# Twelve modulation sums moved from VectorE to GpSimd

## What is computed

```python
def ada_modulate(x, c, norm_g, ada_w, ada_b):
    ada = jax.nn.silu(c) @ ada_w + ada_b          # (1,1024) @ (1024,3072), per layer
    shift, scale, gate = jnp.split(ada, 3, axis=-1)
    h = rmsnorm(x, norm_g) * (1.0 + scale[:, None, :]) + shift[:, None, :]
    return h, gate[:, None, :]

def even_layer(...):
    h, gate_res = ada_modulate(x, c, norm_g, ada_w, ada_b)
    a, u, v, gate = _split(h @ in_w, EVEN_SIZES)
    ya = pool_mixer(a, pool_w, pool_scale)
    yb = spatial_gating(u, v, sgu_norm_g, sgu_w, sgu_b)
    y = jnp.concatenate([ya, yb], axis=-1) * jax.nn.silu(gate)
    return x + gate_res * (y @ out_w)

def odd_layer(...):
    h, gate_res = ada_modulate(x, c, norm_g, ada_w, ada_b)
    gq, gk, gv, glr, sq, sk, sv, gate = _split(h @ in_w, ODD_SIZES)
    ...
```

## Time and profile before

| | |
|---|---|
| median of three runs | 932.27 us (930.97 to 932.85) |
| the profiled execution's own time | 932.22 us |
| its span, first to last instruction | 930.4 us |
| mean granted TensorE clock | 0.994 |
| busy: TensorE / VectorE / ScalarE / GpSimd | 911.9 / 656.7 / 510.3 / 5.8 us |

### The profile page before, as it was taken

One profiled execution on the slowest core, in us unless ns is written; L12 is line 12 of the kernel. 1 busy time (PEld: TensorE's weight loads), 2 busy tenths in 40 slices (PEclk: granted clock), 3 DMA queues, 4 the chain that ended last, 5 costly groups with the idle time before them and its releaser, 6 DMA issues.

```text
span 930.4 us, 19535 instructions
## 1 busy us (share of the span) xinstructions
PE 911.9 (98%) x8637; PEld 887.2 (95%) x8637; DVE 656.7 (71%) x780; ACT 510.3 (55%) x612; POOL 5.8 (1%) x21
## 2 busy tenths in 40 slices
PE   8999999999999999999999999999999999999998
PEld 7999998999999999999998999899899999999998
DVE  3977888785668567767779876557777674465565
ACT  4446353445644567864595663376666553454445
POOL 1000000000000000000000000000000000000000
PEclk9999999999999999999999999999999999999999
DMA  9999457875576634467534443334444566566421
GB/s 337 363 348 322 155 182 263 280 241 171 181 232 221 191 127 137 136 234 227 180 120 149 137 142 92 92 92 148 137 158 137 182 203 215 175 190 215 159 91 46
DMA packets 153559, 172.30 MB, mean 185 GB/s; under 512 B 4152, under 2 KB 137812, under 8 KB 153348
## 3 DMA queue, kind: packets, MB, share of 16 engines
q1 hardware_dynamic: 152032, 168.48, 55.9%
q10 hardware_dynamic: 1220, 2.53, 0.8%
q0 software_dynamic: 224, 0.05, 0.0%
HBM read 170.00 MB, written 1.05 MB: 184 GB/s over the span
## 4 chain that ended last, share of the span: by engine, by line
PE 71%; DVE 12%; ACT 8%; issue 5%; DMA 4%; SPq 0%; DVEq 0%; ACTq 0%
PE pj L2772 57%; DVE w_lo L1557 3%; ACT w_hi L1063 2%; DVE cst_phase L1531 2%; DMA raw<-in_even_in_w_dram 1%; DMA raw<-in_ada_w_dram 1%; PE pj L2724 1%; DMA spare<-in_even_in_w_dram 1%; PE pj L2726 1%; PE pj L2725 1%; PE m_all L2189 1%; PE pj L2555 1%; PE m_all L2462 1%; PE m_all L2445 1%; DMA raw<-in_even_out_w_dram 1%
## 5 line engine op out<-in xcount | busy, mean ns | idle before, releaser
L1557 DVE TENSOR_TENSOR w_lo<-raw,w_hi 128x2048 fp32r<-128x2048 f32 (+2 forms) x129 | 287.9, 2236 | 127.9 <-ACT w_hi L1063 127.2
L2772 PE MATMUL pj<-h_hi,w_hi 128*128 128x256 f32 x1160 | 328.9, 284 | 2.5 <-issue 2.4
L2772 PE MATMUL pj<-h_lo,w_hi 128*128 128x256 f32 x1160 | 323.8, 279 | 0.0
L2772 PE MATMUL pj<-h_hi,w_lo 128*128 128x256 f32 x1160 | 323.7, 279 | 0.0
L1063 ACT ACTIVATE w_hi<-raw 128x2048 fp32r<-128x2048 f32 (+2 forms) x129 | 240.1, 1864 | 53.4 <-PE pj L2772 23.2
L2772 PEld LDWEIGHTS pj<-h_hi,w_hi 128*128 128x128 f32 x1160 | 217.3, 187 | 6.4 <-issue 5.1
L2772 PEld LDWEIGHTS pj<-h_lo,w_hi 128*128 128x128 f32 x1160 | 217.4, 187 | 0.3
L2772 PEld LDWEIGHTS pj<-h_hi,w_lo 128*128 128x128 f32 x1160 | 217.3, 187 | 0.2
L2772 PE MATMUL pj<-y_lo,w_hi 128*128 128x256 f32 x624 | 175.0, 280 | 0.0
L2772 PE MATMUL pj<-y_hi,w_hi 128*128 128x256 f32 x592 | 166.7, 282 | 2.7 <-DVE w_lo L1557 1.9
L2772 PE MATMUL pj<-y_hi,w_lo 128*128 128x256 f32 x592 | 165.8, 280 | 0.0
(11 more groups left out here) (433 smaller groups left out, 1144.9 us busy)
## 6 DMA issues: line engine op xcount, KB each, us to landing
raw<-in_odd_in_w_dram SPq DMA_DIRECT2D x28, 1024.0 KB, 5.2
raw<-in_w_in_dram SPq DMA_DIRECT2D x23, 1024.0 KB, 5.3
raw<-in_ada_w_dram SPq DMA_DIRECT2D x21, 1024.0 KB, 6.4
raw<-in_w_ff_in_dram SPq DMA_DIRECT2D x16, 1024.0 KB, 5.4
raw<-in_w_ff_out_dram SPq DMA_DIRECT2D x16, 1024.0 KB, 5.2
raw<-in_even_in_w_dram SPq DMA_DIRECT2D x12, 1024.0 KB, 5.5
raw<-in_even_out_w_dram SPq DMA_DIRECT2D x8, 1024.0 KB, 6.3
raw<-in_odd_out_w_dram SPq DMA_DIRECT2D x8, 1024.0 KB, 5.4
```

The costliest lines, as they stand in the source:

```text
L1557: V.tensor_tensor(lo[:, 0:n], raw_of(u)[:, 0:n], hi[:, 0:n].bitcast(F32), ALU.subtract).then_inc(done, 1)
L2772: m = nc.tensor.matmul(to, a_, b_, start=(s == 0 and q == 0 and (fb == 0 or not together)), stop=(s == len(steps_) - 1 and q == 2), skip_g ...
```

## The change

A12 to A23 are summed on GpSimd. Where VectorE scaled and added a row block in one instruction, GpSimd is given two: a `tensor_scalar` that multiplies the block in place in `raw`, and a `tensor_tensor` that adds it to `acc`. The first block of an even unit is written to `acc` directly, so an even unit takes seven instructions and an odd one eight, 90 in all; each waits for the one ahead by a new semaphore `ada_pool`. VectorE loses 48 instructions. The SP queue and TensorE wait for `ada_pool` where they waited for `ada_acc`.

```diff
--- before.py
+++ after.py
@@ -48,7 +48,8 @@
 PAD = max(WINDOWS)
 ADA_PE = (0, 2, 4)
 ADA_K, ADA_N = 4, 512
-ADA_DVE = [n for n in range(24) if n not in ADA_PE]
+ADA_POOL = list(range(12, 24))
+ADA_DVE = [n for n in range(24) if n not in ADA_PE and n not in ADA_POOL]
 GLA_H, GLA_C, GLA_TAU = 4, 64, 16.0
 SB_H = 8
 AT_G, AT_H, HD = 3, 4, 64
@@ -724,6 +725,17 @@
             else:
                 eng.wait_ge(S("p_lo"), PLE_LO[un["own"]])
 
+        def ada_pool_ops(n):
+
+            return sum(2 * ADA_K - (m % 2 == 0) for m in ADA_POOL if m <= n)
+
+        def ada_summed(eng, n):
+
+            if n in ADA_POOL:
+                eng.wait_ge(S("ada_pool"), ada_pool_ops(n))
+            else:
+                eng.wait_ge(S("ada_acc"), ADA_DVE.index(n) + 1)
+
         def w_of(un):
 
             if un["own"] is None:
@@ -981,7 +993,7 @@
                         if n in ADA_PE:
                             sp.wait_ge(S("ada_used"), {0: 1, 2: 2, 4: 5}[n])
                         else:
-                            sp.wait_ge(S("ada_acc"), ADA_DVE.index(n) + 1)
+                            ada_summed(sp, n)
                 sp.dma_start(raw_of(u)[:, 0:un["nk"] * un["n"]].rearrange("p (k n) -> p k n", k=un["nk"]),
                              un["src"]).then_inc(unit_sem(u), 16)
 
@@ -1032,6 +1044,25 @@
             pool.memset(a_pad[:, :, 0:PAD], 0.0).then_inc(S("pad_zero"), 1)
             pool.memset(lev[0][:, :, 0:PAD], 0.0).then_inc(S("pad_zero"), 1)
             pool.memset(lev[1][:, :, 0:PAD], 0.0).then_inc(S("pad_zero"), 1)
+            pool_ops = [0]
+            for n in ADA_POOL:
+                u = next(un["order"] for un in units if un["ada"] is not None and un["ada"][2] == n)
+                unit_loaded(pool, u)
+                if n < 20 and n % 2 == 0:
+                    pool.wait_ge(S("ada_used"), n // 2 + 2)
+                w, acc = raw_of(u).rearrange("p (k n) -> p k n", k=ADA_K), acc_of(n)
+                for k in range(ADA_K):
+                    at = ADA_K * (n % 2) + k
+                    if pool_ops[0]:
+                        pool.wait_ge(S("ada_pool"), pool_ops[0])
+                    first = n % 2 == 0 and k == 0
+                    nc.gpsimd.tensor_scalar(acc if first else w[:, k, :], w[:, k, :], silu_c[:, at:at + 1], None, ALU.mult).then_inc(S("ada_pool"), 1)
+                    pool_ops[0] += 1
+                    if not first:
+                        pool.wait_ge(S("ada_pool"), pool_ops[0])
+                        nc.gpsimd.tensor_tensor(acc, acc, w[:, k, :], ALU.add).then_inc(S("ada_pool"), 1)
+                        pool_ops[0] += 1
+                assert pool_ops[0] == ada_pool_ops(n)
             pool.wait_ge(S("rw_cross"), 6)
             pool.wait_ge(S("rw_pairs"), 7)
             for c in range(2):
@@ -1510,7 +1541,7 @@
             def modulation_part(u):
 
                 n = units[u]["ada"][2]
-                if n in ADA_PE:
+                if n in ADA_PE or n in ADA_POOL:
                     return
                 a = ADA_DVE.index(n)
                 unit_loaded(dve, u)
@@ -1518,7 +1549,7 @@
                     dve.wait_ge(S("silu_c"), 1)
                 if n in (5, 6):
                     dve.wait_ge(S("ada_used"), n - 2)
-                elif 8 <= n < 20 and n % 2 == 0:
+                elif n in (8, 10):
                     dve.wait_ge(S("ada_used"), n // 2 + 2)
                 elif n % 2:
                     dve.wait_ge(S("ada_acc"), a)
@@ -2687,7 +2718,7 @@
                     pe.wait_ge(S("silu_c"), 1)
                     w = raw_of(u).rearrange("p (k n) -> p k n", k=ADA_K)
                 else:
-                    pe.wait_ge(S("ada_acc"), ADA_DVE.index(n) + 1)
+                    ada_summed(pe, n)
                 for fb in range(4):
                     cols_ = slice(fb * P, (fb + 1) * P)
                     if n >= 8:
```

## The result

The changed kernel takes 1000.63 us (median of four runs, 1000.01 to 1001.87) against 932.44 us (930.97 to 932.85) for the kernel before, run beside it. The ratio is 1.0747, with a 95% interval of 1.0732 to 1.0763: 68 us slower. Forecast were 948 us and a range up to 966. The sign was right, the size was not.

What follows compares the result with a forecast made beforehand. TensorE, 98% busy, bounds the kernel; its gate and out stage is fed just in time by places freed in `raw`. Span 930.4 plus 15.4 there, other places 0, and 1.8 outside the span: 947.6, rounded to 948 us; range 935 to 966.

Steps and rivals of the forecast that it cites:

- T16: Gate and out stage: moment unit A16 gives its place in `raw` back, forecast at 175.0 us.
- the price: Cost of one GpSimd instruction on 128 x 512: 1.0 us undisturbed, halfway between full overlap and no overlap of reads and writes.
- The floor: Lower end of the GpSimd instruction price: reads and writes overlap fully, one stream as in a memset row, 0.62 us.
- additions longer than scalings: Sign expected in the next profile's GpSimd rows if the forecast was right, with GpSimd busy near 100 us.
- The factor of 1.3 for the meetings: Gate and out stage: VectorE's two-input work beside GpSimd raises an instruction from 1.0 to 1.3 us.
- rival 4: GpSimd much slower, over 1.6 us an instruction; at 2.0 the stage loses 38 us, 980 us in all; chance 0.10.
- T22: Odd layer: moment unit A22 gives its place in `raw` back; forecast 296.9 us, or 311.5 at 2.0 us an instruction.
- The steps from T13 to T19: Gate and out stage: unit-by-unit times at which A13 to A19 free their places in `raw`; stage ends 15.4 us late.
- Two ordinary units and the norm ahead: Behind the gate and out stage: work ahead of the unit needing A19's place, taken as cover, so A19 costs 0.
- 5.5 us of cover: Odd layer: the unit behind A22 is split at 306.7 us, TensorE starts on it at 312.24, so the delay costs 0.
- A12 at 0: GpSimd ends A12 by 84.6 us, the next unit could be split at 92.3, VectorE took it at 92.17: no loss.
- The half clock: Gate and out stage: TensorE runs at granted 0.50 after each wait for a late split; 1.8 us more behind each later one.

Runs made afterwards that it cites:

- the pair of runs with and without reads: Kernel before plus GpSimd work nobody waits for: the 90 scalings and additions, 962.36 us; each replaced by three memsets of 128 x 512, 932.64 us.
- the run of memsets: Kernel before, all sums on VectorE, plus three GpSimd memsets of 128 x 512 for each of 90 instructions, nobody waiting: 932.64 us, ratio 1.0011.

## Why the prediction was wrong, step by step

**The direction was right.** VectorE's relief bought nothing, and the places in `raw` set the pace, as said. GpSimd's rounds (T16 to T17 20.4 us, T17 to T18 17.3, T18 to T19 21.1) are far longer than two jobs of TensorE (11.2). The sum gave the span 15.4 us more, and it grew by 68.3. The missing 52.9 are 23.3 in the gate and out stage (38.7 measured), and 7.1 behind A12, 12.9 at the norm and 12.0 in the odd layer, all three priced at 0, less the 2.4 that came back.

**The failed step is the price**, "I take it, since the two ends are equally far from any row": 1.0 us bare, where 1.5 was measured. The floor came from a write row; a scaling turned out dearer than two streams in sequence (1.57 against the 1.14 that the forecast had as its upper end), and only the addition lay inside its bounds (1.27 of at most 1.66). The sign "additions longer than scalings" came out reversed (1.65 and 1.97). The factor of 1.3 for the meetings was right in size, 1.92 / 1.5 is 1.28, but partly by luck. Its upper end was worked out wrong: if GpSimd is kept out for 33 of 80 us, it has 47 left for the same work, and 1.0 becomes 1.7, not 1.4. Both together are the forecast's rival 4, "much slower". Its sum was wrong too: at 2.0 us the steps give T18 = 235.3 and E3b's split at 246.9, a loss of 44.6 us and not 38 (and T22 = 312.3), so 983 to 986 us. At the measured 1.92 they give 41, and 38.7 were measured. That rival had a chance of 0.10 and its price lay outside the range, because I bounded an unseen instruction by memsets.

**The steps from T13 to T19 held**, as far as these runs can tell. The run without additions lost 6.9 us in the stage where they give 6.3 for its price, with the waits spread otherwise and an error of some 3 us on such a shift. In the full change T16 came at 198.5 instead of 175.0: 7.1 us from A12, 18.6 from 30 instructions at 1.92 instead of 1.3, less the 2.3 us pause between A13 and A14 that went.

**"Two ordinary units and the norm ahead" was no cover.** A19 was priced at 0; the norm lost 12.9 us, and taking A19 alone off GpSimd gives back 10.2. I had asked when TensorE needs the unit. What decides is what stands behind that unit's rounding and split on ScalarE and VectorE: here the squares and `x` of the norm. At the forecast's price the norm still loses 5.4 us, part of which the run of memsets lost as well (3.6).

**The odd layer's "5.5 us of cover" failed in the same way**, +12.0 in the change and +13.2 alone: TensorE missed not the late unit but the recurrence's VectorE work queued behind its split. Two things had to be wrong here, the place where the cover was counted and the price: with the additions left out nothing is lost.

**A12 at 0** cost 7 us. With A12's end at the measured 91.5 us the same 7.65 us of transfer and rounding put the next split at 99.1 us, against 92.17, and it began at 100.06: the step was right, the price again was not.

**The half clock** came, but not behind every wait: granted 0.50 between 170 and 171 us, behind the split of 164.87 and a wait of 2.0 us, and 1.00 between 195 and 196, behind a wait of 1.46 us. **Disturbance**: the forecast's sign for it, one instruction with two lengths, is there (1.57 and 4.00). The rule on SBUF's interference that it cited (the Trainium skill, SBUF — State Buffer, section Who interferes with whom) agrees with the pair of runs with and without reads: 751 ns rise to 1137 with reads and stay at 752 without. The estimate of 7.6 us for eight instructions, from the figures of the Trainium skill, GPSIMD Engine Reference (section Elementwise — side-by-side cycle accounting), was too low; 12.1 were measured undisturbed. The addition that the Trainium skill gives there, a quarter of 4497 ns, is near the 1.27 us of this trace; the Trainium skill's 769 ns for 512 elements in the best case is far from the 1.49 to 1.57 us of a scaling.

## What to carry to other kernels

Ask of a unit that comes late not when its consumer needs it, but what stands behind its own preparation in each in-order queue: at A19 and in the odd layer, where I had counted on cover, that is what stopped first. A price for an instruction that no row shows needs a range that a run of eight such instructions would narrow at once; memset rows are no bound for instructions that read. An engine that is idle by the page is not free: here GpSimd's reading instructions slowed VectorE's two-input instructions even when nobody waited for their result. And a wait removed at one job can come up at the job ahead of it, so look at both.

## What the runs showed of the hardware that I had not expected

GpSimd scales 128 x 512 float32 in 1.57 us but adds two such tensors in 1.27, and multiplies by a broadcast column in 1.04. Copying takes 0.61.

90 GpSimd instructions for which nobody waits cost the kernel 30.6 us (962.36 against 931.76), while 270 memsets, which keep GpSimd busy for four fifths as long (150.8 us beside 184.9), cost nothing that can be measured. Yet memsets are not quite without effect: over the stretch from 50 to 450 us VectorE's `TENSOR_SCALAR` that begins a sum in `acc` rose from 481 to 561 ns, and a cast of 128 x 256 from 295 to 485, while the two-input forms stayed.
